# Expert layers: the combination becomes the tail of the experts' stage, and the router's weights are split in the projection before

## The reference

```python
def _layer_norm(x, g, b):
    mu = jnp.mean(xf, -1, keepdims=True)
    var = jnp.mean(jnp.square(xf - mu), -1, keepdims=True)
    return (xf - mu) * lax.rsqrt(var + LN_EPS) * g + b

def _hierarchical_moe(x, w_rg, b_rg, w_re, b_re, w_gate, w_up, w_down):
    g_logits = xf @ w_rg + b_rg                       # 4 groups
    g_w, g_idx = lax.top_k(jax.nn.softmax(g_logits, axis=-1), 1)
    e_logits = ...                                    # 8 experts of the chosen group
    e_w, e_idx = lax.top_k(jax.nn.softmax(e_logits, axis=-1), MOE_TOP_K)
    gates = g_w * e_w / jnp.sum(e_w)
    ...
    h = jax.nn.silu(xb @ w_gate[e]) * (xb @ w_up[e])  # for the rows of expert e
    y = h @ w_down[e]
    # y of a token: the sum of its two experts' rows, weighted by gates

for i in range(DEPTH_2):
    x = _layer_norm(DEEPNORM_ALPHA * x + mix, ln_g[i, 0], ln_b[i, 0])
    ffn = _hierarchical_moe(x, ...)
    x = _layer_norm(DEEPNORM_ALPHA * x + ffn, ln_g[i, 1], ln_b[i, 1])
```

## Time and profile before

| | us |
|---|---|
| median of 3 runs | 3463.43 (3453.08 to 3473.08) |
| the profiled execution | 3459.48 |
| its span | 3457.6 |
| PE busy | 2988.7 (86%) |
| DVE busy | 1150.9 (33%) |
| ACT busy | 860.7 (25%) |
| POOL busy | 466.6 (13%) |

### The profile page before, as it was taken

The page is one execution under the profiler, slowest core; times in us unless marked ns, Lnnn a source line. Parts: engine busy times, 40 slices in busy tenths (PEclk is TensorE's granted clock), DMA queues, the critical chain, the costliest instruction groups (busy, mean ns, idle before and its releaser), DMA issues. The chain is left out here.

```text
span 3457.6 us, 40987 instructions
## 1 busy us (share of the span) xinstructions
PE 2988.7 (86%) x15735; PEld 2121.1 (61%) x15735; DVE 1150.9 (33%) x1827; ACT 860.7 (25%) x1739; POOL 466.6 (13%) x666
## 2 busy tenths in 40 slices
PE   7998989899989999999898688888499876888883
PEld 6777769777778878788776333333288753333331
DVE  3554754333353333346454200000353552000002
ACT  2514841332233310124541111111211431111112
POOL 0122510000000000000440011111122310111110
PEclk9998999999999999999799799899699987988897
DMA  3242023133333322221012899999443018999995
GB/s 124 86 102 74 2 74 95 41 86 86 85 97 97 97 83 94 91 79 51 1 62 87 354 382 403 402 392 401 169 129 97 21 52 346 367 401 397 390 406 198
DMA packets 250615, 605.22 MB, mean 175 GB/s; under 512 B 39829, under 2 KB 204051, under 8 KB 225788
## 3 DMA queue, kind: packets, MB, share of 16 engines
q1 hardware_dynamic: 238268, 583.05, 46.4%
q0 software_dynamic: 10880, 16.83, 1.4%
q10 hardware_dynamic: 1344, 3.67, 0.5%
HBM read 596.61 MB, written 24.16 MB: 180 GB/s over the span
## 5 line engine op out<-in xcount | busy, mean ns | idle before, releaser
L2745 PE MATMUL bank<-moe_raw,ex_xT 128*64 128x512 f32 x1984 | 526.9, 691 | 150.7 <-DMA moe_raw<-in_moe_w_up 147.7
L2745 PEld LDWEIGHTS bank<-moe_raw,ex_xT 128*64 128x64 f32 x1984 | 187.0, 158 | 444.4 <-issue 436.5
L2840 DVE TENSOR_TENSOR ex_h<-ex_gate,bank 64x512 f32<-64x512 f32 x64 | 44.1, 690 | 988.9 <-ACT ex_gate L2803 988.9
L248 PE MATMUL bank<-hT_hi,cut_lo 128*128 128x512 f32 x1248 | 313.1, 393 | 0.0
L248 PE MATMUL bank<-hT_hi,ahead 128*128 128x512 f32 x624 | 259.0, 415 | 28.0 <-DVEq L421 17.8
L248 PEld LDWEIGHTS bank<-hT_hi,cut_lo 128*128 128x128 f32 x1248 | 234.8, 188 | 53.0
L248 PE MATMUL bank<-hT_lo,ahead 128*128 128x512 f32 x624 | 257.0, 412 | 0.0
L248 PE MATMUL bank<-hT_hi,cut_hi 128*128 128x512 f32 x624 | 245.2, 393 | 1.1 <-DVE cut_hi L277 1.1
L248 PE MATMUL bank<-hT_lo,cut_hi 128*128 128x512 f32 x624 | 245.0, 393 | 0.0
L2762 PE MATMUL bank<-moe_raw,ex_hT 128*64 128x512 f32 x992 | 225.2, 593 | 1.3 <-ACT ex_hT L2807 1.3
L2803 ACT ACTIVATE ex_gate<-bank 64x512 f32<-64x512 f32 x64 | 37.8, 590 | 664.1 <-PE bank L2745 664.1
(11 more groups left out here) (564 smaller groups left out, 5327.5 us busy)
## 6 DMA issues: line engine op xcount, KB each, us to landing
moe_raw<-in_moe_w_gate SPq DMA_DIRECT2D x62, 2048.0 KB, 14.0
moe_raw<-in_moe_w_up SPq DMA_DIRECT2D x62, 2048.0 KB, 18.5
moe_raw<-in_moe_w_down SPq DMA_DIRECT2D x62, 2048.0 KB, 9.6
raw<-in_w_in SPq DMA_DIRECT2D x26, 1024.0 KB, 5.4
raw<-in_w_ffn_in SPq DMA_DIRECT2D x44, 512.0 KB, 5.0
raw<-in_ssd_w_in SPq DMA_DIRECT2D x20, 1024.0 KB, 5.3
raw<-in_attn_w_qkv SPq DMA_DIRECT2D x18, 1024.0 KB, 5.0
raw<-in_w_in SPq DMA_DIRECT2D x24, 512.0 KB, 4.4
```

Of the source, the lines that this page charges most:

```text
L248: last = nc.tensor.matmul(out, a(pa, k), b(pb, k), start=(late == "hi" and k == 0 and n == 0), stop=(late == "lo" and k == kt - 1 and n == ...
L2745: last = nc.tensor.matmul(GU[s][rows, :], xT[:, s, k * ER:(k + 1) * ER], raw[slot][which][:, k * HID:(k + 1) * HID], start=(k == 0), stop= ...
L2840: nc.vector.tensor_tensor(h[:, s, :], gate[:, s, :], GU[s][right, :], ALU.mult).then_inc(h_ready, 1)
```

## The change

The router's weights get a class of their own (`Router`). They are loaded behind g and b of the norm in the projection's stage, and POOL splits them there, into a place in SBUF that is kept free for them. (For this the projection of layer 1 puts its own parts where the attention's q and k were.) The routing stage no longer loads or splits them: PE's product has no wait before it, and ACT waits for the two biases instead of DVE.

The combination is no stage any more. Its instructions follow the experts' loop in the same stage on each engine. SP loads g and b after the last expert's weights, waits itself for the last scatters, and issues the picked rows. These lie where slot 0 of the weights was. POOL still waits for the scatters too. ACT has no scaling any more; instead DVE multiplies x by ALPHA once, all four tiles in one instruction at the head of the experts' stage, and then adds both experts' rows with their weights, one instruction each.

```diff
 class Router:
+    def loads(self, sp):
+        A, layer = self.A, self.layer
+        sp.dma_start(self.whole[:, :, 0:EG], A.moe_w_router_group_2[layer]...).then_inc(self.loaded, 16)
+        sp.dma_start(self.whole[:, :, EG:], A.moe_w_router_expert_2[layer]...).then_inc(self.loaded, 16)
+    def split(self, pool):
+        nc, cut = self.nc, self.cut
+        pool.wait_ge(self.loaded, 32)
+        nc.gpsimd.tensor_copy(cut.hi[:, :, :], self.whole[:, :, :]).then_inc(self.rounded, 1)
+        pool.wait_ge(self.rounded, 1)
+        nc.gpsimd.tensor_tensor(cut.lo[:, :, :], self.whole[:, :, :], cut.hi[:, :, :].bitcast(F32), ALU.subtract).then_inc(self.is_split, 1)
 class LayerNormTail:
     def loads(self, sp):
...
+        if self.router:
+            self.router.loads(sp)
 def moe_route(...):
-                sp.dma_start(wr[:, :, 0:EG], A.moe_w_router_group_2[layer]...).then_inc(loaded, 16)
-                sp.dma_start(wr[:, :, EG:NL], A.moe_w_router_expert_2[layer]...).then_inc(loaded, 16)
             def _(pe):
-                pe.wait_ge(is_split, 1)
             def _(act):
+                act.wait_ge(loaded, 32)
                 act.wait_ge(product_ready, 1)
             def _(dve):
-                dve.wait_ge(loaded, 64)
-                split_weights(nc, dve, wr[:, :, :], cut.hi[:, :, :], cut.lo[:, :, :], rounded, 1).then_inc(is_split, 1)
 def moe_experts(...):
+            def mix(dve, t, done):
+                if t == 0:
+                    dve.wait_ge(x_scaled, 1)
+                dve.wait_ge(K.picked[2 * t], 16)
+                nc.vector.scalar_tensor_tensor(out=K.x[:, t, :], in0=picked[:, 0, t, :], scalar=weight[:, 0, t:t + 1], in1=K.x[:, t, :],
+                                               op0=ALU.mult, op1=ALU.add).then_inc(summed, 1)
+                dve.wait_ge(K.picked[2 * t + 1], 16)
+                dve.wait_ge(summed, t + 1)
+                return nc.vector.scalar_tensor_tensor(out=K.x[:, t, :], in0=picked[:, 1, t, :], scalar=weight[:, 1, t:t + 1], in1=K.x[:, t, :],
+                                                      op0=ALU.mult, op1=ALU.add, accum_out=tail.total[:, t:t + 1])
             def _(sp):
...
+                tail.loads(sp)
+                for s in range(2):
+                    sp.wait_ge(y_stored[s], n * 16 + 16)
+                sp.sem_inc(asked, 1)
+                rows = K.y_rows.rearrange("(h q) c -> q h c", h=2)
+                for t in range(TT):
+                    for k in range(2):
+                        sp.dma_start(picked[:, k, t, :].rearrange("p (h c) -> p h c", h=2),
+                                     rows[k * S + t * P:k * S + (t + 1) * P]).then_inc(K.picked[2 * t + k], 16)
+                if K.opening:
+                    K.opening.begin(sp)
...
             def _(act):
...
+                tail.scalar(act, None)
             def _(dve):
+                nc.vector.tensor_scalar(K.x[:, :, :], K.x[:, :, :], ALPHA, None, ALU.mult).then_inc(x_scaled, 1)
                 with dve.Fori(0, pairs_used(dve)) as i:
...
+                tail.vector(dve, None)
-def moe_combine(nc, K, A, layer, weight, tail):
...
```

More of the change, by code:

```diff
@@ L703, in tensor, with __init__ @@
                 turn_tile(self.nc, self.K, self.term[:, t, :], t).then_inc(turned, 1)
+class Router:
+    def __init__(self, nc, K, A, layer):
+        self.nc, self.A, self.layer = nc, A, layer
+        words = KD * (EG + NE)
+        first = nc.sbuf_top - 8 * KD * P - 3 * 4 * words
+        at = lambda n, part, dtype: nc.alloc_sbuf_tensor_at(f"router{layer}_{part}", [P, KD, EG + NE], dtype, offset=first + 4 * n * words)
+        self.whole = at(0, "whole", F32)
+        self.cut = Names()
+        self.cut.hi, self.cut.lo = at(1, "hi", F32R), at(2, "lo", F32R)
+        self.loaded, self.rounded, self.is_split = (nc.alloc_semaphore(f"router{layer}_{n}") for n in ("loaded", "rounded", "is_split"))
+    def loads(self, sp):
+        A, layer = self.A, self.layer
+        sp.dma_start(self.whole[:, :, 0:EG], A.moe_w_router_group_2[layer].rearrange("(k p) m -> p k m", p=P)).then_inc(self.loaded, 16)
+        sp.dma_start(self.whole[:, :, EG:], A.moe_w_router_expert_2[layer].rearrange("(k p) m -> p k m", p=P)).then_inc(self.loaded, 16)
+    def split(self, pool):
[4 more added lines that the diff above has]
+        nc.gpsimd.tensor_tensor(cut.lo[:, :, :], self.whole[:, :, :], cut.hi[:, :, :].bitcast(F32), ALU.subtract).then_inc(self.is_split, 1)
 class LayerNormTail:
     names = ("g_loaded", "mixed", "centred", "squared", "varied", "rooted", "inverted", "shifted", "normed", "turned", "rounded", "split")
-    def __init__(self, mem, nc, K, g_row, b_row, dst, sort=False):
+    def __init__(self, mem, nc, K, g_row, b_row, dst, sort=False, router=None):
+        self.router, self.on_pool = router, router and router.split
         sb = lambda n, s: mem.enter_context(nc.sbuf_tensor(f"ln_{n}_{nc.next_id()}", s, F32))
         self.nc, self.K, self.g_row, self.b_row, self.dst, self.sort = nc, K, g_row, b_row, dst, sort
-        self.g, self.b, self.junk = sb("g", [P, D]), sb("b", [P, D]), sb("sq", [P, D])
+        self.g, self.b = sb("g", [P, D]), sb("b", [P, D])
+        self.junk = sb("sq", [P, D]) if K.tail_junk is None else K.tail_junk
         self.total, self.mean, self.square, self.var, self.std, self.rstd = (sb(n, [P, TT]) for n in ("total", "mean", "square", "var", "std", "rstd"))
@@ L2457, in moe_route @@
         NL = EG + NE
-        wr, br = sb("w", [P, KD, NL]), sb("b", [NL, 1])
-        cut = Pair(mem, nc, f"rt{layer}_cut", [P, KD, NL])
+        br, cut = sb("b", [NL, 1]), K.router.cut
         lgT, lg = sb("logitT", [NL, S]), sb("logit", [P, TT, NL])
@@ L2660, in store_rows, with moe_experts @@
                                  in_=y[:, s, :], in_offset=None, bounds_check=4 * S - 1, oob_is_err=False).then_inc(K.y_stored[s], 16)
-def moe_experts(nc, K, A, layer, expert, pairs, idx, place, raw, x, y, to):
+def moe_experts(nc, K, A, layer, expert, pairs, idx, place, raw, x, y, to, weight, picked, tail):
     weights_d = expert_weights(A, layer)
@@ L2691, in _ @@
                 load(5, 5, 0, 4)
-                with sp.Fori(3, pairs_used(sp)) as i:
+                n = pairs_used(sp)
+                with sp.Fori(3, n) as i:
                     for s in range(2):
@@ L2695, in _ @@
                         load(b, sp.value_load(expert[0:1, ds(b, 1)], min_val=0, max_val=NE - 1), 1 - s, b - 1)
+                tail.loads(sp)
[9 more added lines that the diff above has]
+                    K.opening.begin(sp)
+                if tail.dst is None:
+                    for t in range(TT):
+                        sp.wait_ge(normed, t + 1)
+                        sp.dma_start(K.out[t * P:(t + 1) * P, :], K.x[:, t, :]).then_inc(out_stored, 16)
+                    sp.wait_ge(out_stored, 16 * TT)
             @block.gpsimd
```

83 lines of the change are left out of this document (26 added, 57 removed).

## The result

The changed kernel takes 3435.6 us (median of six runs, 3433.8 to 3444.3) where the kernel before takes 3465.1 us in six runs (3453.1 to 3473.1). The ratio is 0.9917, with a 95% interval of 0.9897 to 0.9937: 29 us faster, 0.83%. Forecast were 3435.0 us and 28.0 us. The profiled execution has a span of 3431.8 us against 3457.6, and its granted clock is 0.915 of full speed against 0.913.

What follows compares the result with a forecast made beforehand. The weights' stream was taken to bound the loops, which the change leaves alone. Gains of 11.6, 12.9 and 8.5 less 0.4, 3.8 and 0.8 gave 28.0 us: 3431.5 profiled, 3435 as median, range 3422 to 3449 (8 in 10).

Steps and rivals of the forecast that it cites:

- Term 1: Behind the experts' loops: SP issues picked rows without the barrier, 6.0 us earlier in layer 1, 5.6 in layer 0, sum 11.6.
- Term 2: Start of the combination's norm: first landing to first normed tile takes 8.6 us instead of 14.8 and 15.3, sum 12.9.
- Term 3: Head of the routing: with the router's split ahead, PE starts 4.5 and 4.0 us earlier, sum 8.5 us.
- Term 4: Head of the experts' stage: DVE's new scaling of x holds POOL back 1.9 us a layer, a loss of 3.8 us.
- Rival (a): Head of the experts' stage: POOL isn't held by DVE's scaling, so the sum is 31.8 us, 3431.6; chance 0.13.
- Term 5: End of the program: 12 more semaphores to clear at 0.065 us each, a loss of 0.8 us, visible once.
- Rival (b): Head: an earlier gather still lands only when the weights' backlog clears, so nothing is won there; sum 23.3, 3440.1; chance 0.18.
- Rival (d): Experts' loops: moved code makes jumps back fetch instructions; slower beyond 6 us a jump, 3491 at 7 us; chance 0.04.

## Why the prediction was right

**Term 1** (11.6 us): 12.0 measured between the two events, and 11.7 when the barrier was put back. Right in mechanism and size: SyncE sees the scatters when POOL does, and the DRAIN runs beside the norm. The sign named for it, a first picked issue within 0.3 us of the DRAIN's start, holds in layer 1 only. In layer 0 POOL comes to its DRAIN 16.9 us later, by way of the next stage's weights, which the prediction had not followed.

**Term 2** (12.9 us): 12.2 from the first issue, 11.4 from the first landing. From the landing to the first normed tile it takes 9.2 and 9.6 us, not 8.6: the second tile's rows come 3.64 (layer 0) and 4.05 us (layer 1, 3407.99 - 3403.94) behind the first's, not the 2.83 taken from the earlier trace rows, and DVE's list has their additions ahead of the first tile's scaling. What the prediction did not say is how this term is built: its working took away both waits together, and by the runs that put one of them back, neither removal alone would have been worth more than 1.3 us in a layer (12.61 and 12.95 with neither, 18.2 and 17.8 with ACT's, 19.6 and 19.1 with g and b's, 19.5 and 18.2 with both).

**Term 3** (8.5 us): 9.1, since PE starts 0.32 us behind hT.lo, where 0.65 were allowed. The split on POOL takes 0.42 + 0.80 us in layer 0 and 0.72 + 1.66 in layer 1, there a little more than the bound of two instructions of 1.04, and ends 26 to 35 us before the last hT.lo does: it is hidden.

**Term 4** (-3.8 us): the mechanism right, the size too large. The scaling takes 2.29 us, not 2.6. It begins with the clears, and POOL reaches its copy 0.83 and 1.14 us behind its start, about as forecast. But the copy then ends with the scaling, while the forecast let it run its own 0.2 us behind that end, so 1.3 and 1.0 us are lost in the layers, -2.4 in all. The Trainium skill (SBUF — State Buffer, section "SBUF: two separate sides") says that a VectorE instruction in a 2-port mode locks GpSimd out, descriptors too. The trace agrees in both halves: the copy of 1.51 us ends with the scaling (1932.69 and 1932.64), and the issue beside the second scaling takes 2.24 us and ends 0.88 us behind it (1940.63 and 1939.75). That GpSimd gets in between two such instructions is seen here as well. Rival (a), that POOL isn't held, falls.

**Term 5** (-0.8 us): 27 clears take 1.6 us from first to last start, 15 took 1.0; behind the last tile it is 0.76 us longer.

**Rival (b)** was right on where the gather's time goes and wrong on what follows from it. With the weights held the gather needs 3.1 and 3.7 us, so 5 to 6 us are spent beside them; but its duration doesn't depend on when it is issued while the backlog lasts (8.4 and 10.1 before, 9.1 and 9.8 with the router part alone). The Trainium skill (DMA: Bandwidth & Descriptors, section "Queues, rings and completion order") has each DMA engine go round its queues packet by packet. The trace agrees in this: with the scaling moved the gather has landed at 1947.25, while the stream stays full until about 1954.7 (0.34 of the window from 1953), so it doesn't wait for all that is queued ahead. That the 5 to 6 us are such turns with the stream is not shown by a row. **Rival (d)**, slower loops, falls: their length is within the scatter named above.

The measured terms sum to 12.0 + 12.2 - 0.5 + 9.1 - 2.4 - 0.8 = 29.6 us (0.5 is the table's row of the other three tiles, forecast as 0.4), where the forecast had 28.0: term 4's error is the largest. The profiled pair shows 25.8, above all because the two loops came out 2.7 us longer in sum (5.3 longer and 2.6 shorter) and the stages ahead of the experts 2.7 us (3.8 longer and 1.1 shorter); the medians show 29.5. Part of the exact hit is luck: the changed kernel's own runs lie between 3424.7 and 3444.3.

## What to carry to other kernels

When a barrier is in the way, look at what its slowest member does in it: here POOL's DRAIN behind the last software DMA took 5.46 us, and could run beside the next work, which only needed the data. Where an engine waits twice in a row, work out each removal alone as well: here two edits together won about 6 us a layer, and either alone would have won at most 1.3. A small transfer that work waits for can be worth a pause of the large stream: here the gather came 5 to 6 us earlier and the kernel was some 13 us faster; and large VectorE copies or scalings belong where GpSimd has nothing to issue.

## What had not been expected of the hardware

- The DRAIN behind the last scatter has a fixed length, with the transfers landed: 5457 ns in layer 1 of every kernel profiled, and 5462 ns in layer 0 of the three that have a barrier there. Where POOL's cast of the next weights comes first (layer 0 without the barrier), the DRAIN starts with the cast and lasts as long as it and 5.5 us more: 8297 ns beside a cast of 2.80 us, and 7391 ns beside one of 1.89 in the changed kernel's other profile. It starts 20 us behind the last scatter's issue there, so the 5.5 us are not the time of a landing. In the kernel before, whose barrier had a DRAIN between the scatters and the cast, the DRAIN beside the cast lasts 2592 ns and the cast 2.51 us: the 5.5 us are paid once. What POOL does in them is not shown. Not all its DRAINs are of this length: behind the two software DMAs of the routing they take 11.1 to 12.7 us, beside 36 us of work of the other engines.
- POOL's cast and a DVE addition beside it stretch the addition in layer 0: 2.72 us in the kernel before, 2.91 in the changed kernel and 2.96 when it was run again, where it takes 1.28 otherwise. That is 1.4 to 1.7 us on DVE, which neither kernel avoids.
- A backlog of one load (2 MB) beside the gather costs it more than half of what three cost: 7.1 and 6.9 us to PE, against 8.8 and 8.9 with all three, and 3.1 and 3.7 with none.
